# A hybrid encoder block on eight cores: other durations in the model that orders its instructions

## The reference

```python
u = rms_norm(x, g_pre)
c_b, c_c, c_x, c_z, q, k, v, r, lr_f, lr_b, m_a, m_b = split(u @ w_in)
# mixer A: a gated convolution over three positions
p_conv = (c_b * conv3(c_c * c_x, conv_w) * silu(c_z)) @ w_out_c
# mixer B: gated linear attention in both directions, 4 heads, keys of 128, values of 256
g = log_sigmoid(lr @ w_gate + b_gate) / 16          # one for each direction
o = gla(q, k, v, g_f, forward) + gla(q, k, v, g_b, backward)
p_gla = (rms_norm_per_head(o) * silu(r)) @ w_out_g
merged = sigmoid(m_a) * p_conv + sigmoid(m_b) * p_gla
y = x + rms_norm(merged @ w_out, g_post)
```

## Time and profile before

| | us |
|---|---|
| median of three timed executions | 2944.9 |
| lowest of the three | 2936.92 |
| the profiled execution: time | 2938.5 |
| its span on the slowest core (core 6) | 2936.9 |
| spans of the eight cores | 2916.5 to 2936.9 |
| TensorE busy on core 6 | 2799.3 |
| VectorE busy | 1984.0 |
| ScalarE busy | 1593.3 |
| GpSimd busy | 1069.0 |

### The profile page before, as it was taken

The page is one execution under the profiler, slowest core; times in us unless marked ns, Lnnn a source line. Parts: engine busy times, 40 slices in busy tenths (PEclk is TensorE's granted clock), DMA queues, the critical chain, the costliest instruction groups (busy, mean ns, idle before and its releaser), DMA issues.

```text
span 2936.9 us, 53943 instructions; the slowest of 8 cores (2916.5 to 2936.9 us)
## 1 busy us (share of the span) xinstructions
PE 2799.3 (95%) x15502; PEld 1480.5 (50%) x15740; DVE 1984.0 (68%) x2905; ACT 1593.3 (54%) x2973; POOL 1069.0 (36%) x1405
## 2 busy tenths in 40 slices
PE   5898998999999999999999999999999999999998
PEld 3455544444456664444446665444445666544443
DVE  4667676576577677567667777657767767756665
ACT  5565764433566775443456686443356677543243
POOL 3656465242232234135142323325323323412422
PEclk9987998999999999999999999999999999999999
DMA  8997965484563224375464322448466222344445
GB/s 206 201 172 174 175 173 153 154 263 150 183 176 78 64 67 105 129 225 173 151 203 112 77 68 65 125 145 257 140 180 185 75 69 64 93 133 154 135 138 171
DMA packets 370976, 423.01 MB, mean 144 GB/s; under 512 B 220528, under 2 KB 252272, under 8 KB 370176
## 3 DMA queue, kind: packets, MB, share of 16 engines
q1 hardware_dynamic: 361760, 402.56, 47.8%
q0 software_dynamic: 8928, 16.98, 4.1%
HBM read 324.65 MB, written 65.60 MB: 133 GB/s over the span
## 4 chain that ended last, share of the span: by engine, by line
PE 82%; DVE 4%; DMA 4%; issue 3%; SPq 3%; ACT 2%; POOL 1%; DVEq 0%; POOLq 0%; ACTq 0%
PE ps L492 82%; SPq L552 2%; DMA sb_KT<-sb_GR 1%; SPq L549 1%; DVE sb_CS L522 1%; DMA sb_W<-wst 1%; DMA sb_onT<-x 1%; DVE sb_GR L518 1%; DMA wst<-sb_OS 1%; DMA sb_W<-wsc 1%; ACT sb_CS L509 0%; DVE sb_AT L518 0%; DVE sb_CS L518 0%; DVE sb_TF L522 0%; DMA sb_uT<-sb_ycT 0%
## 5 line engine op out<-in xcount | busy, mean ns | idle before, releaser
L492 PE MATMUL ps<-sb_uT,sb_W 128*128 128x512 bf16 (+3 forms) x7518 | 1585.1, 369 | 25.8 <-DVE sb_CS L518 5.5
L492 PEld LDWEIGHTS ps<-sb_uT,sb_W 128*128 128x128 bf16 (+1 forms) x7680 | 729.5, 98 | 768.9 <-issue 71.2
L509 ACT ACTIVATE sb_CS<-ps 128x512 f32<-128x512 f32 (+3 forms) x544 | 304.3, 568 | 268.1 <-PE ps L492 240.2
L518 POOL TENSOR_TENSOR sb_GR<-sb_CS 128x512 bf16<-128x512 f32 x128 | 166.4, 1302 | 645.1 <-DVE sb_CS L522 639.8
L492 PE MATMUL ps<-sb_GR 128*128 128x512 bf16 (+2 forms) x1766 | 349.0, 319 | 3.6 <-POOL sb_GR L518 2.0
L492 PE MATMUL ps<-sb_GR,sb_W 128*128 128x512 bf16 x1054 | 261.2, 379 | 8.5 <-ACT sb_LR L509 5.9
L522 DVE SCALAR_TENSOR_TENSOR sb_CS<-sb_CS,sb_convw 128x512 f32<-128x512 bf16 x256 | 249.5, 985 | 15.6 <-ACT sb_CS L509 5.5
L518 POOL TENSOR_TENSOR sb_CS<-sb_CS 128x512 f32<-128x512 f32 x128 | 169.2, 1324 | 213.1 <-DVE sb_CS L522 181.7
L492 PE MATMUL ps<-sb_W,sb_uT 128*128 128x256 bf16 x2048 | 243.6, 278 | 0.0
L518 DVE TENSOR_TENSOR sb_CS<-ps,sb_CS 128x512 f32<-128x512 f32 (+3 forms) x288 | 180.9, 628 | 88.6 <-PE ps L492 51.3
L492 PEld LDWEIGHTS ps<-sb_GR 128*128 128x128 bf16 x1792 | 165.2, 99 | 142.0 <-issue 7.0
(11 more groups left out here) (159 smaller groups left out, 3749.3 us busy)
## 6 DMA issues: line engine op xcount, KB each, us to landing
sb_W<-wsc SPq DMA_DIRECT2D x272, 256.0 KB, 2.9
sb_W<-wst SPq DMA_DIRECT2D x128, 512.0 KB, 4.3
sb_W<-wst SPq DMA_DIRECT2D x128, 384.0 KB, 3.3
sb_onT<-x SPq DMA_DIRECT2D x50, 512.0 KB, 6.4
sb_GR<-x SPq DMA_DIRECT2D x40, 512.0 KB, 5.7
sb_OS<-w_pairs SPq DMA_DIRECT2D x32, 512.0 KB, 4.9
y<-sb_GR SPq DMA_DIRECT2D x32, 512.0 KB, 3.1
sb_ycT<-x SPq DMA_DIRECT2D x32, 512.0 KB, 5.5
```

The lines of the kernel that those rows point to most:

```text
L492: S.add("pe", lambda e: e.matmul(out, lhsT=lhsT, rhs=rhs, start=start, stop=stop, skip_group_check=skip), r, w, cost=max(0.025, free_n(rhs ...
L509: S.add("act", lambda e: e.activation(out=out, in_=in_, func=func, **kw), r, w, table=TABLE.get(func), cost=0.17 + 0.82e-3 * free_n(in_) + ...
L518: S.add(eng, lambda e: e.tensor_tensor(out=out, in0=a, in1=b, op=op), r, w, cost=ecost(eng, free_n(out), narrow(out, a, b)))
```

## The change

Six durations in the model get other values, and `CROWD`, the weight of the surcharge above, goes from 0.1 to 0.05. No instruction is added or removed apart from the choices that hang on the model.

```diff
--- before.py
+++ after.py
@@ -124,7 +124,7 @@
                         slack = d.end + MARGIN
             self.starts.append((eng, slack, t))
         if semkey is not None:
-            self.free[eng] = ready + hold + (1.0 if eng == "pool" else 0.0)
+            self.free[eng] = ready + hold + (0.55 if eng == "pool" else 0.0)
             d0 = max(self.free["dma"], ready)
             self.free["dma"] = d0 + nbytes / DMA_RATE
             op.end = self.free["dma"] + DMA_LAT
@@ -340,7 +340,7 @@
 TOL = 0.02
 BACKLOG = 3.0
 FULL = 4.0
-CROWD = 0.1
+CROWD = 0.05
 IDLE = 2.0
 GRAN = 256
 
@@ -507,12 +507,12 @@
             if accum is not None:
                 kw["accum_out"] = accum
             S.add("act", lambda e: e.activation(out=out, in_=in_, func=func, **kw), r, w, table=TABLE.get(func),
-                  cost=0.17 + 0.82e-3 * free_n(in_) + (0.2 if accum is not None else 0.0))
+                  cost=0.17 + 0.82e-3 * free_n(in_) + (0.2 if accum is not None else 0.0) + (0.12 if scale is not None and not isinstance(scale, float) else 0.0))
 
         def ecost(eng, n, fast):
             if eng == "pool":
-                return 0.45 + 1.63e-3 * n
-            return 0.15 + (0.52e-3 if fast else 1.04e-3) * n
+                return 0.3 + 2.0e-3 * n
+            return 0.15 + (0.63e-3 if fast else 1.04e-3) * n
 
         def tt(eng, out, a, b, op, r, w):
             S.add(eng, lambda e: e.tensor_tensor(out=out, in0=a, in1=b, op=op), r, w,
@@ -520,10 +520,10 @@
 
         def stt(out, in0, scalar, in1, op0, op1, r, w):
             S.add("dve", lambda e: e.scalar_tensor_tensor(out=out, in0=in0, scalar=scalar, in1=in1, op0=op0, op1=op1), r, w,
-                  cost=0.21 + 1.05e-3 * free_n(out))
+                  cost=0.21 + 1.05e-3 * free_n(out) + (0.23 if in0.dtype == BF16 else 0.0))
 
         def ts(eng, out, in0, s1, s2, op0, op1, r, w):
-            c = 0.2 + 1.15e-3 * free_n(out) if eng == "pool" else ecost(eng, free_n(out), narrow(out, in0))
+            c = 0.27 + 1.0e-3 * free_n(out) if eng == "pool" else ecost(eng, free_n(out), narrow(out, in0))
             S.add(eng, lambda e: e.tensor_scalar(out=out, in0=in0, scalar1=s1, scalar2=s2, op0=op0, op1=op1), r, w, cost=c)
 
         def cp(eng, out, in_, r, w, scale=None):
@@ -538,7 +538,7 @@
         def evac(out, in_, r, w, scale=None, engs=("act", "dve")):
 
             n = free_n(out)
-            cost = {"act": 0.17 + 0.82e-3 * n, "dve": ecost("dve", n, narrow(out, in_)), "pool": 0.2 + 1.15e-3 * n}
+            cost = {"act": 0.29 + 0.82e-3 * n if scale is not None else 0.17 + 0.82e-3 * n, "dve": ecost("dve", n, narrow(out, in_)), "pool": 0.2 + 1.15e-3 * n}
             eng = min(engs, key=lambda e: max(S.free[e], S.free["pe"]) + cost[e])
             cp(eng, out, in_, r, w, scale)
 
@@ -696,7 +696,7 @@
 
         def rsqrt(out, in_, eps, n, r, w, np_=128):
             ts("pool", out, in_, eps, 1.0, ALU.add, ALU.mult, r, w)
-            S.add("pool", lambda e: e.tensor_tensor(out=out, in0=out, in1=cst[0:np_, 0:n], op=ALU.pow), w + ["cst"], w, cost=0.6)
+            S.add("pool", lambda e: e.tensor_tensor(out=out, in0=out, in1=cst[0:np_, 0:n], op=ALU.pow), w + ["cst"], w, cost=0.7)
 
         def rs_stat(ms, msk, np_=128):
             rsqrt(ms[0:np_, 2:3], ms[0:np_, 0:1], EPS, 1, msk, msk, np_)
```

## The result

The changed kernel takes 2986.6 us (median; 2982.55 in its lowest execution) against 2944.9. The ratio is 1.0155, with a 95% interval of 1.0109 to 1.0200: slower by 1.1 to 2.0 per cent, and on the other side of the forecast. Some executions of any kernel are slower on one half of the chip, so every ratio here is of undisturbed executions, and where a run has no ratio, its profiled time is given.

The account below looks back on a forecast made before the run. TensorE was taken as the bound, busy 2799.3 of 2936.9 us. The terms -7.1 + 9.2 - 2.9 - 6.9 = -7.7 us took 2944.9 to 2937.2 us; the 8-in-10 range was 2906 to 2982.

Parts of the forecast that it names:

- Part 4: Attention parts of batches 1 to 3: 5.7 us gained, 3.4 lost a batch; -6.9 us in all, bounds -23 and +16.5.
- two dense steps: Fourth head, batches 1 to 3: two steps with only 1.1 us of matmuls take 2.8 us each; 3.4 lost a batch.
- Part 1: First forward product in batch 0: the 7.06 us wait for transposed keys goes; gain 7.1 us, bounds 0 and 9.
- Part 2: End of batch 0's first head: TensorE falls behind VectorE's denser work; loss 9.2 us, bounds 0 and 17.
- Part 3: Fourth head of batch 0: VectorE's work exceeds TensorE's by 7.2 us instead of 10.1; gain 2.9 us.
- heads 2 and 3: Batch 0: they come out even, taken at 0; the third is tight and may cost up to 5 us.
- slower rival: VectorE bounds dense steps: batch 0's first and fourth heads, later batches' fourth; +31 us, 2976 us; chance 0.23.
- The remark that the added 0.23 us for taps: VectorE's taps: the new model spreads a wait for GpSimd evenly over taps, most without it; if so, sum 6.9 us higher.
- my signs: Right if batches 1 to 3 take 698 to 700 us; wrong if dense steps cost over 2.8 us each.

Follow-up runs that it names:

- The run with batch 0 held: The changed kernel with three convolution items of batch 0 held back, so nine pieces stand behind its first head's first step; ratio 1.0168, profiled 2976.5 us.

## Why the prediction was wrong

**Part 4 is the step that failed first.** I took its waits' end for granted (5.7 a batch) against a loss of 3.4 at two dense steps, -6.9 in all. Measured is +23.7, beyond the bound of +16.5. By place: the first head, priced at -4.0 a batch, costs +3.2; the fourth head's steps, priced at +3.4 less the 1.7 of the earlier trace rows, cost +3.1; and +3.5 stand behind the fourth head, to which I gave nothing. Three things were missing. The dense step was priced at the 2.8 us that one took in the earlier trace rows, by TensorE's rows; it also has three transposes on SyncE, 3.6 us, and in the trace VectorE waits for them through the buffers of `ON`, as TensorE does for the weights behind them. The waits that I expected to go were named by their last releaser, and did go under that name (`CS`, `TF`), but came back as `SB` by GpSimd, 7.6 for 3.3. And I gave the clock nothing here, since the attention parts of these batches had no fall in the earlier trace rows; it is about half of the 8 us.

**Part 1 failed as told, and its sum came near by luck.** The wait for the keys didn't go but moved to 82.22 us, 7.25 us long, and one for `uT` of 7.05 stands behind it. I had looked at what is late at the old place and not at what the new one waits for. Counted to the first head's first product, 4.2 us were gained on core 7 (5.5 in the median of six cores) of the 7.1, but not at the place that I named; where they come from was not followed up.

**Part 2 held.** The first head of batch 0 waits 8.14 and 7.18 us for `SB` where it waited 9.69, and its seven intervals take 51.7 us for 25.4 of work, against 47.8 for 37.5. Counted as the prediction counts, to the next head, the loss is 6.2 us on core 7 and 5.1 in the median, where I took 9.2 with bounds of 0 and 17.

**Part 3 failed beside the place that it priced.** The fourth head gains 0.8 us and not 2.9. But of heads 2 and 3 I said that they come out even, at most 5 us late, and took 0; there 2.6 and 20.1 us are lost (6.9 and 19.8 in the median). My working compared VectorE's load with TensorE's in each head, 82.5 beside 84.0 us in the third, as if a head could be as short as the larger of the two. It took 110 us, as it had before with 104.8 us of TensorE's work in it. The loss isn't load: gates, scan and key products follow each other across engines, and the work that used to cover them had been spent earlier, 21 us of it in this head. This term, taken at 0, is 26.7 us in the median, more than all of batch 0's +25.0. The run with batch 0 held shows the same from the other side: there the first two heads lose less, and the third 33.7 us where the changed kernel loses 25.5 and the kernel before 5.7 (medians).

**The sum and its neighbours.** The slower rival (2976, its case 2955 to 3000) was nearest: dense steps whose line isn't covered by TensorE work. Its size is right, but partly by luck: of its 31 us the third head had 5, and 20 were lost there, and VectorE is only a part of it beside SyncE's transposes and the chain between heads. It stood at 0.23 behind a forecast that rested on small gains. The range ended 4.6 us below the measured time, since its bounds took each part's loss from one engine. The remark that the added 0.23 us for taps is a mean that no tap has was borne out in the rows (median 0.750 after too) but was not the cause alone: with all prices left as they were the halved surcharge costs 29.4 us, and with the taps cut short the difference stays. Of my signs, the batch period of 709 us in place of 698 to 700 showed the failure. The dense steps did not: in batch 1's fourth head the two took 1.1 and 3.0 us on core 7, and the one behind them 6.9 for 2.8 of work. Where TensorE's order is the same, behind the last step of batch 0, nothing is lost.

**What stays open.** The loss is settled by place, and the longest waits of the changed order have their chains in the trace. Which number causes it is not a question with one answer here: the parts don't add up, and neither sign is safe. Whether orders as good as the old one are rare or only far from these eight sets of numbers, the runs don't tell. That SyncE's queue heads the chains of the first head and of the late weights is read from traces; it wasn't tried with a third buffer, fewer transposes or another queue. That the third head's length in batch 0 is set by a chain and not by load is a reading too; no run moved its gate products alone. Nor was ScalarE's part tried alone.

## What to carry to other kernels

When a greedy scheduler's order has few waits left, truer durations in its model can be a new draw and no improvement, as here: measure some neighbours of the old numbers, in both directions, before believing a reason for one. Price a dense step by every queue that it uses, the one that issues its DMAs among them, and price the gap that its filler work was taken from: a head that takes 110 us with 105 us of work in it may take 110 with 84. And where TensorE runs without a fall of its clock, a few new waits of 1 to 4 us can cost twice their length, as here.

## What the runs showed of the hardware

- In the changed kernel a fall of the granted clock to 0.50, for 3.4 or 6.8 us, came with waits of 0.8, 0.5 to 1.0 and 1.7 us close together (on core 7 in batch 1 from 1174.6 to 1178.5) in 24 of 24 cases (eight cores, batches 1 to 3), and with the one wait of 3.6 to 3.9 us in the first head in 22 of 24. Short waits in a row did as much to the clock as a long one; why two of the long ones had no fall stays open.
- A DMA transpose of 128 by 256 elements holds SyncE's queue for some 1.2 us (4.93 us for four, 7.53 for six), against 0.3 to 0.5 us for a plain load of weights.
- A GpSimd copy of 256 columns takes 0.48 us alone and 1.35 beside VectorE's taps on 512 columns; beside taps on 16 columns it takes 0.48 again.
